# A streaming encoder layer on one core: gate exponentials placed elsewhere in ScalarE's order, tables of the second group in eight buffers between weight slabs, four product stores, one norm buffer per tile

## The reference, cut to what matters

```python
proj = x @ w_in                                   # q | k | v | u, 1024 columns each
att  = band attention of 16 heads over q, k, v    # with a learned bias on distance
ssm  = s5(u)                                      # 64 groups x 64 complex states, GELU, gate
mix  = concat(rmsnorm(att), rmsnorm(ssm)) @ w_out
x1   = layer_norm(alpha * x + mix)
# expert layer: 8 heads, 128 x 128 product keys, 16 experts of each head for each token
q    = x1 @ wq ; s = q . keys
idx  = top 16 of (top 16 of s1 + top 16 of s2) ; g = softmax of these 16 scores
a    = einsum('td,tkd->tk', x1, peer_u[idx])      # 128 dot products of 2048 for each token
y    = einsum('tk,tkd->td', gelu(a) * g, peer_v[idx])
x2   = layer_norm(alpha * x1 + y)
```

## Time and profile before

| | us |
|---|---|
| median of three runs | 4193.71 |
| the profiled execution's own time | 4181.71 |
| its span | 4179.8 |
| TensorE busy (L1418 slabs 1036.9, L1728 products 906.0) | 2642.1 |
| VectorE busy (rows: L1251 1042.8 and 296.5, L1238 724.3) | 2805.5 |
| GpSimd busy | 1239.6 |
| ScalarE busy | 345.2 |
| moved by DMA | 1334.30 MB, mean 319 GB/s |

### The profile page before, as it was taken

One profiled execution on the slowest core, in us unless ns is written; L12 is line 12 of the kernel. 1 busy time (PEld: TensorE's weight loads), 2 busy tenths in 40 slices (PEclk: granted clock), 3 DMA queues, 4 the chain that ended last, 5 costly groups with the idle time before them and its releaser, 6 DMA issues.

```text
span 4179.8 us, 31056 instructions
## 1 busy us (share of the span) xinstructions
PE 2642.1 (63%) x11464; PEld 2042.3 (49%) x11464; DVE 2805.5 (67%) x3300; ACT 345.2 (8%) x808; POOL 1239.6 (30%) x1386
## 2 busy tenths in 40 slices
PE   7989989989668677892988499970999500000000
PEld 6868577845454344551557477860887400000000
DVE  4350211389873888778779886298066598999998
ACT  0110221000001212101010000000000001000000
POOL 2440000012231222222222222023022256777772
PEclk9975579989559555895999799985999855555555
DMA  8653144488996899997999799698699998999997
GB/s 239 223 176 86 58 153 165 149 262 314 353 408 236 311 351 354 373 422 289 422 422 398 313 422 412 230 401 336 209 391 423 400 393 300 409 410 410 408 409 331
DMA packets 291063, 1334.30 MB, mean 319 GB/s; under 512 B 69536, under 2 KB 129472, under 8 KB 139488
## 3 DMA queue, kind: packets, MB, share of 16 engines
q0 software_dynamic: 140432, 952.56, 57.2%
q1 hardware_dynamic: 110384, 365.54, 23.9%
q10 hardware_dynamic: 40096, 14.22, 1.7%
HBM read 1284.43 MB, written 57.20 MB: 321 GB/s over the span
## 4 chain that ended last, share of the span: by engine, by line
DMA 34%; DVE 25%; PE 25%; issue 8%; POOL 6%; ACT 1%; ACTq 1%; SPq 0%; DVEq 0%; POOLq 0%
DMA arena<-in_peer_v,arena 20%; PE low L1418 10%; DVE arena L1238 7%; DVE acc L1251 7%; DMA expert_scratch<-arena 6%; PE low L1728 4%; POOL arena L572 3%; DMA arena<-c_scratch 3%; POOL arena L563 3%; PE low L1522 2%; DMA arena<-in_w 2%; PE low L1506 1%; PE acc L1481 1%; DVE low L1251 1%; DMA arena<-in_peer_u,arena 1%
## 5 line engine op out<-in xcount | busy, mean ns | idle before, releaser
L1251 DVE SCALAR_TENSOR_TENSOR acc<-arena,acc 128x2048 f32<-128x2048 f32 x443 | 1042.8, 2354 | 269.0 <-DMA arena<-in_peer_v,arena 247.3
L1418 PE MATMUL low<-arena 128*128 128x192 f32 (+1 forms) x4096 | 1036.9, 416 | 56.6 <-DMA arena<-in_w 36.0
L1728 PE MATMUL low<-arena 128*128 128x256 f32 x4096 | 906.0, 383 | 232.6 <-ACT arena L800 178.1
L1728 PEld LDWEIGHTS low<-arena 128*128 128x128 f32 x4096 | 779.2, 191 | 359.3 <-issue 193.1
L1418 PEld LDWEIGHTS low<-arena 128*128 128x128 f32 x4096 | 742.2, 195 | 342.3 <-issue 33.6
L563 POOL DMA_INDIRECT arena<-in_peer_v,arena x576 | 558.5, 970 | 1061.8 <-DVE acc L1251 790.5
L1238 DVE SCALAR_TENSOR_TENSOR arena<-arena,acc 128x2048 f32<-128x2048 f32 x320 | 724.3, 2284 | 79.1 <-DMA arena<-in_peer_u,arena 72.7
L563 POOL DMA_INDIRECT arena<-in_peer_u,arena x320 | 320.9, 1003 | 1464.8 <-DVE arena L1238 981.5
L1251 DVE SCALAR_TENSOR_TENSOR low<-arena,low 128x2048 f32<-128x2048 f32 x126 | 296.5, 2353 | 18.4 <-DMA arena<-in_peer_v,arena 15.4
L572 POOL DMA_INDIRECT arena<-expert_scratch,arena x256 | 248.0, 969 | 77.9 <-issue 77.9
L1196 DVE TENSOR_REDUCE arena<-arena 128x8 f32<-128x128 f32 x5 | 1.4, 284 | 236.8 <-ACT arena L780 236.8
(11 more groups left out here) (265 smaller groups left out, 2044.7 us busy)
## 6 DMA issues: line engine op xcount, KB each, us to landing
arena<-in_w SPq DMA_DIRECT2D x128, 1024.0 KB, 6.2
arena<-in_ut SPq DMA_DIRECT2D x128, 1024.0 KB, 17.7
expert_scratch<-arena SPq DMA_DIRECT2D x128, 128.0 KB, 15.0
arena<-bias_scratch SPq DMA_DIRECT2D x16, 640.0 KB, 5.6
arena<-in_peer_v,arena POOLq DMA_INDIRECT x576, 12.2
arena<-toeplitz_scratch SPq DMA_DIRECT2D x64, 128.0 KB, 4.8
arena<-c_scratch SPq DMA_DIRECT2D x64, 128.0 KB, 5.4
bias_scratch<-distance_scratch POOLq DMA_DIRECT2D x1, 5120.0 KB, 25.7
```

The costliest lines, as they stand in the source:

```text
L1251: stt(held, slot[j], wv_, held, ALU.mult, ALU.add).then_inc(used, 1)
L1418: ins = mm(L[n % 2][:, 0:width], wring[n % 2][:, k, :], rhs(k), start=k == 0, stop=k == KT - 1)
L1728: ins = mm(L[j % 4][:, 0:NSD], ud[j % 4][:, k, :], lane(catB, k)[:, P:NB], start=k == 0, stop=k == KT - 1)
```

## The change

It reorders and rebuffers; no arithmetic is added or left out. `gates(t)`, `gate(t)` and `activated` stand at other places of their lists, and the GELU of tile 2 is split in two halves. Group B's state tables (and group A's) get eight buffers, their pairs are done in blocks of four (increments) and eight (output) between slabs. The product store has four stage buffers. Layer norm 1 of group B has a buffer for each tile, with all three inputs loaded ahead; the last norms and sums stand elsewhere.

```diff
+PARTS = [(0, 0, KK), (1, 0, KK // 2), (2, 0, KK // 2), (2, KK // 2, KK // 2)]
...
-        tab = [at(H5 + 512 * j, 512) for j in range(4)]
+        tab = [at(o_ + 512 * j, 512) for o_ in (H5, H6 + D) for j in range(4)]
-        x1s = [at(H8, D), at(H7, D), xhatB, xhatB, xhatB]
+        x1s = [at(H8, D), at(H7, D), xhatB, at(H6, D), at(H6 + D, D)]
-        astg = [at(H2 + D + NSD * j, NSD) for j in range(2)]
+        astg = [at(H2 + D + NSD * j, NSD) for j in range(4)]
@@ SP @@
-            weights(N_VB + 4, 2)
-            for g in range(GP):
+            for g in range(8):
                 g_table(g)
-            weights(N_VB + 6, 2)
+            for b in range(6):
+                if b:
+                    for g in range(4 * b + 4, 4 * b + 8):
+                        g_table(g)
+                if b < 4:
+                    weights(N_VB + 4 + b, 1)
+                else:
+                    weights(N_KB + b - 4, 1)
...
             sp.wait_ge(s_done, 2 * GP)
-            for g in range(4):
+            for g in range(8):
                 y_tables(1, g)
-            weights(N_KB, 8)
+            weights(N_KB + 3, 3)
+            for b in range(3):
+                for g in range(8 * b + 8, 8 * b + 16):
+                    y_tables(1, g)
+                if b < 2:
+                    weights(N_KB + 6 + b, 1)
             weights(N_QB, 2)
-            for g in range(4, GP):
-                y_tables(1, g)
...
-            tokens(2, xinB)
+            for t in range(NGA, NT):
+                tokens(t, x1s[t])
             sp.dma_start(keysB, a["keys_t"]).then_inc(keys_in, 16)
             weights(N_MB + 2, 16)
-            for t in (3, 4):
-                sp.wait_ge(xin_free, t)
-                tokens(t, xinB)
...
+                if j == EB - 12:
+                    early_sums()
@@ ScalarE @@
-            for i in range(8):
+            for i in range(4):
                 out_of(N_KB + i, kT[:, i, NA:T], L[i % 2][:, 0:NB])
-            for b in range(8):
-                act.wait_ge(y_done[1], 4 * b + 4)
+            for b in range(4):
+                act.wait_ge(y_done[1], 8 * b + 8)
...
+                out_of(N_KB + 4 + b, kT[:, 4 + b, NA:T], L[b % 2][:, 0:NB])
-            y_store(1, 8, yscrB, U8B)
-            gates(1)
+            y_store(1, 4, yscrB, U8B)
             act.wait_ge(y_done[1], GP)
-            for i in range(8):
+            for i in range(6):
                 out_of(N_QB + i, qB[:, i, :], L[i % 2][:, 0:NB], DH ** -0.5)
             act.wait_ge(yd_ready, 2)
             nc.scalar.activation(yB, yB, ACT.Gelu).then_inc(gelu_done, 1)
+            for i in range(6, 8):
+                out_of(N_QB + i, qB[:, i, :], L[i % 2][:, 0:NB], DH ** -0.5)
...
+                if v == 4:
+                    gates(1)
...
-            products(0, 12)
+            products(0, 40)
             gates(2)
-            products(12, 60)
+            products(40, 92)
+            activated(2)
+            products(92, EB)
+            activated(3)
             gates(3)
-            products(60, 72)
-            activated(2)
-            products(72, 92)
             gates(4)
-            products(92, EB)
-            ln2(0, 2)
+            ln2(0, 0)
+            ln2(1, 1)
             chunk(0)
             chunk(1)
-            ln2(1, 0)
-            ln2(2, 1)
+            ln2(2, 2)
@@ VectorE @@
             decode(0, nothing)
-            for h in range(PH):
-                rows(2)
-                head(1, h)
-            decode(1, rows)
-            rows(2)
+            rows(36)
...
-            rows_to(72)
-            gate(0)
-            rows_to(96)
-            gate(1)
+            for h in range(PH):
+                rows(3)
+                head(1, h)
+            rows(2)
             dve.wait_ge(y_moved[1], 16)
...
+            dve.wait_ge(y_done[1], GP)
+            decode(1, rows)
+            rows_to(96)
...
+                if v == 8:
+                    gate(0)
+                if v == 16:
+                    gate(1)
...
-            rows(64)
+            rows(50)
             for t in range(NGA, NT):
-                ln1(t, xinB, xhatB, lngB, lnbB, low, rows)
+                ln1(t, x1s[t], x1s[t], lngB, lnbB, low, rows)
                 rows(2)
-            rows(60)
+            rows(50)
             for h in range(PH):
-                rows(min(left // PH, 4))
+                rows(5)
                 head(2, h)
             decode(2, rows)
             rows_to(R_U2 + 4)
-            gate(2)
             for t in (3, 4):
                 for h in range(PH):
                     rows(5)
                     head(t, h)
                 decode(t, rows)
-                rows(8)
-                if t == 3:
-                    gate(3)
-            rows(16)
-            gate(4)
-            rows_to(R_V3)
+            rows_to(R_V2)
+            gate(2)
+            rows_to(R_V2 + KK // 2)
+            gate(3)
+            gate(4)
+            rows(4)
+            dve.wait_ge(early_in, 80)
...
+            ln2(0, 0, rows)
+            rows()
+            ln2(1, 1, rows)
+            rows_to(R_V3 + 4)
+            ln2(2, 2, rows)
@@ TensorE @@
-            for g in range(GP):
-                if g % 4 == 0 and g >= 8:
-                    pe.wait_ge(y_out[1], g // 4 - 1)
...
+            for b in range(4):
+                if b:
+                    pe.wait_ge(y_out[1], b)
+                for g in range(8 * b, 8 * b + 8):
+                    c0 = 1024 + CB * (g % 8)
+                    y_pair(1, g, [low[:, c0 + 512 * g2:c0 + 512 * g2 + CB] for g2 in range(2)], U8B, HsB, CB)
+                slab(N_KB + 4 + b, xb, NB)
...
             for t in range(NGA, NT):
                 if t > NGA:
-                    pe.wait_ge(x1t_out, 4 * t)
+                    pe.wait_ge(res_ready, t)
                 residual(t, mixB, NA, low)
-                pe.wait_ge(res_ready, t + 1)
+            pe.wait_ge(res_ready, NT)
+            for t in range(NGA, NT):
                 turned(t, L[0:2])
```

More of the change, by code:

```diff
@@ L301, in build @@
         k_done, k_out, s_done, s_out = (sem(n) for n in ("k_done", "k_out", "s_done", "s_out"))
-        g_in = [sem(f"g_in{j}") for j in range(4)]
+        g_in = [sem(f"g_in{j}") for j in range(8)]
         t_made = [sem(f"t_made{j}") for j in range(2)]
         h_ready = sem("h_ready")
-        y_in = [sem(f"y_in{j}") for j in range(4)]
+        y_in = [sem(f"y_in{j}") for j in range(8)]
         y_done, y_out, y_stored, y_moved = (
@@ L331, in build @@
         ud_used, a_out = sem("ud_used"), sem("a_out")
-        a_st = [sem(f"a_stored{j}") for j in range(2)]
+        a_st = [sem(f"a_stored{j}") for j in range(4)]
         ln2_in, early_in, late_in = sem("ln2_in"), sem("early_sums_in"), sem("late_x1_in")
@@ L399, in _ @@
                 pair_in(0, m)
-            for g in range(4, GP):
+            for g in range(8, GP):
                 y_tables(0, g)
@@ L497, in _ @@
                 sp.dma_start(x1f[t], x1scr[t]).then_inc(late_in, 16)
-            for k, t in enumerate((2, 0, 1, 3, 4)):
+            for t in range(NT):
                 t0, n = TILES[t]
-                sp.wait_ge(y_ready, k + 1)
+                sp.wait_ge(y_ready, t + 1)
                 sp.dma_start(o["y"][t0:t0 + n, :], x1f[t][0:n]).then_inc(outs, 16)
@@ L586, in _ @@
             pool.wait_ge(idx_ready, NT)
-            for b in range(2):
-                pool.wait_ge(a_st[b], 16 * EB // 2)
+            for b in range(4):
+                pool.wait_ge(a_st[b], 16 * EB // 4)
             for k in range(16):
@@ L770, in scores @@
                 src = acc if t < NGA else low
-                if t == NT - 1:
+                if t == NGA:
                     act.wait_ge(x1_stored, 16 * NT)
@@ L894, in _ @@
                 out_of(N_MB + i, mixB[:, i, :], L[i % 2][:, 0:NB])
-            for t in range(NGA, NT):
-                ln1_stats(t, xhatB)
-                ln1_out(t)
+            ln1_stats(2, x1s[2])
+            ln1_stats(3, x1s[3])
+            ln1_out(2)
+            ln1_stats(4, x1s[4])
+            ln1_out(3)
+            ln1_out(4)
             slabs_out(N_WB, 16, mixB, NB)
@@ L1631, in _ @@
                 slab(N_UB[q], xb, NB)
-            for i in range(6):
+            for i in range(2):
                 slab(N_VB + i, xb, NB)
             pe.wait_ge(u_moved[1], 16 * SL)
-            for g in range(GP):
-                pe.wait_ge(g_in[g % 4], 16 * (g // 4 + 1))
-                if g % 4 == 0 and g >= 8:
-                    pe.wait_ge(s_out, GP + g // 4 - 1)
-                for r in range(2):
-                    for g2 in range(2):
-                        c0 = 2 * CB * (g % 4) + CB * r
-                        ins = mm(L[2 + (g // 4) % 2][hf(g2), c0:c0 + CB],
-                                 GTb[g % 4][:, P * r + 64 * g2:P * r + 64 * g2 + 64], U8B[:, 2 * g + g2, :],
-                                 start=True, stop=True)
-                ins.then_inc(s_done, 1)
-            for i in range(6, 8):
```

(28 more changed lines are left out.)

130 lines of the change are left out of this document (65 added, 65 removed).

## The result

The changed kernel took **4035.37 us** (median of 4 runs, 4029.42 to 4040.64), the kernel before 4193.31 us beside it on the same chip: a ratio of 0.9623 [0.9607, 0.964], 158 us less. Five more runs on another chip gave 4035.59 us and 0.9608 [0.9594, 0.9622]. The forecast was 4000 us in a range from 3935 to 4100, so 35 us too low.

A forecast was written before the change was run, and what follows sets the result against it. DMA was taken to bound the stretch from products to row 640, with stalls from ScalarE's order. Row 640 at 3308 plus a 678 us tail made 3986, -194 us against 4180; from 4193.7 that gave 4000 us, range 3935 to 4100.

The forecast's parts named there:

- The mechanism: From products to row 640: ScalarE's list asks too early and delivers too late, stopping VectorE and TensorE; 208 us lost before.
- The sum in bytes: First product to row 640: 497 MB at 422 GB/s, 1177 us, plus 28 us loss; row 640 at 3308, -188 us.
- rival 1: Half of the 208 us loss comes back at other waits of VectorE's list: +76 us, 4076 us; chance 0.17.
- The first failed step: Between first product and row 640, sums, x1 and norm vectors counted only as about 6.6 MB of loads.
- 128 products take about 890 us: Product stretch: with four stores, neither stores nor four-buffer loads pace TensorE, so the products take about 890 us.
- it covers the wait at row 576: Four stores keep products ahead of VectorE's row 576 (about 3105); at 7.75 us each they would end at 3095.
- Rival 4: Products starve and VectorE stands at row 576 until the last; slower from 9.5 us a product; chance 0.03.
- The start of attention and of the products: Stages before the products: attention 28 us earlier, products at 2103 instead of 2174, 71 us earlier.
- The tail: Behind row 640: two of three norms and three sums leave, so 684 us become 678.
- the forecast's last step: Total: the -194 us from the span is taken from the median 4193.7, 12 us above the profiled execution, giving 4000 us.
- Rival 3: DMA gives only 358 GB/s: row 640 at 3490, the run at 4185 us, no gain; chance 0.04.
- Rival 2: Pairs at 2.4 GHz (-17), none of the 28 us loss stays, scores' wait covered: about 3940 us; chance 0.10.

The follow-up runs named there:

- run 1: Kernel before with only ScalarE's list reordered, the GELU of tile 2 halved and gates 2 to 4 at their new rows; ratio 0.9609.
- Run 4: Changed kernel with two stage buffers and two product stores in flight instead of four; 4036.78 us, ratio 0.9623 to the kernel before.
- run 8: Changed kernel with 14 rows moved ahead of VectorE's wait for the state output and its gating at row 106, not 96; ratio 0.9602 to the kernel before.
- Runs 2 and 5: Kernel before with the norm buffers' part alone, ratio 1.005; kernel before with the state tables' part alone, GELU unsplit, ratio 1.001.
- tables_clean: Kernel before with the state tables' part alone: eight buffers, pairs in blocks between slabs, GELU unsplit, picks unmoved; ratio 1.001.
- gates_only: Kernel before with only ScalarE's new order, the halved GELU of tile 2 and the gates' new rows; ratio 0.9609.

## Why the prediction was right, and where it was not

**The mechanism** was as put: ScalarE's list stopped VectorE and TensorE in turn, and its order is the gain (run 1: 0.9609, 164 of 4200 us; the whole change 158 to 165). The four waits of the earlier trace rows are gone, and none of VectorE for the exponentials took their place.

**The sum in bytes.** 497 MB were forecast from 2103 to row 640; the window gives 1226 us at 406 GB/s, 498 MB. At 422 GB/s that is 1180 us. 28 us of loss were left in the sum; 46 were there. By 422 less what each window shows: 10 us at 2998 to 3060, 18 at 3121 to 3200 (sums and norms, 15 forecast), 15 at 3280 to 3329 (double gathers, 8 forecast), 3 over the rest. The decodes, 5 forecast, lost nothing: they lie before 2998 us, and DMA moved 423 GB/s from 2103 to 2601 and 422 from 2601 to 2998. Row 640 came at 3329 and not 3308. One term of the sum for the kernel before was off: it has 298 rows left at 2174 us, but by its row instructions row 345 ran there, so 295 were left, and its windows give 359 GB/s x 1322 us = 475 MB and not 470. That makes its loss 197 us and not 208; of the forecast only rival 1's price hangs on it.

**The first failed step** is the loads of the early sums, which the sum had only as bytes. They stand in SP's list ahead of slab 117, and TensorE's timeline shows the price:

```profile
2998.31 7.17 PE L1759 MATMUL low<-arena 128*128 128x256 f32 x32 [2.13 <-DMA arena<-in_ut]
3035.58 22.65 PE L1759 MATMUL low<-arena 128*128 128x256 f32 x96 [30.10 <-DMA arena<-in_ut]
```

30.10 us without a slab, and the fourth window of the result has the DMA engines full (1.01) but moving 355 GB/s.

**The second** is "128 products take about 890 us": they took 1018. I took 6.95 us for one from a stretch where the rows stood and laid the 7.75 beside flowing rows to the store. Run 4 shows that it isn't: beside flowing rows a product takes 7.75 us with two stores or four, and TensorE waits for slabs, 112 to 114 us in all. 128 x 7.75 us and the stop of 30 above make the 1018 within some us. Only "it covers the wait at row 576" hung on it, and the sign "products 128 x about 7 us without a gap", which did not come. That cover was nearly gone: last product 3121.0, row 576 at 3132.0, forecast 2995 and 3105. It cost the changed kernel nothing and the next one 33 us (run 8). Rival 4's 9.5 us a product was the price at which all the gain is lost; the waiting begins at (3132 - 2103)/128 = 8.0 us.

**The start of attention and of the products** came out by their steps. `h_ready` 1073 (forecast 1069); pairs and four slabs 1073 to 1214, 141 us (141); query slabs' end 1303 (1296); skip term 1236.9 (1239); gating 1313.4 (1317); layer norm 1 in 53 us (54); the slabs behind it at 1909.7 (1908); first product 2102.6 (2103). But the wait of 49.7 us at L1351 was in the step only by its end and not as a wait: with its slots full, DMA ran at 135 GB/s, a loss of (422 - 135)/422 x 50 = 34 us by bytes that the sum did not see, because it counted from 2103. Run 8 took 23 us off that wait.

**That these marks are worth nothing alone** follows from the sum, since an earlier start with rows owed moves the same bytes; the prediction had the eight and 25 rows owed, but it never said that 71 us earlier products are only a few us of time. Runs 2 and 5 show it: 35 and 31 us earlier at the products, and 20 and 1 us later at row 640.

**The tail** took 699 us and not 678. The order there is not the reason: all the kernels in the table but one have 698 to 703 us, `tables_clean` with the tail of the kernel before among them, and the one with 683 is the profiled execution of before. GpSimd's 468 instructions behind row 640 took 452.20 us in it and 478.72 in `gates_only`, which has the same tail. So the forecast took the tail from an execution whose tail was short; why it was short is not shown. That execution was 12 us below its median, which the forecast's last step added to the total, so if those 12 us lie in the tail, they were in the forecast after all. So the span is off by 42 us (21 + 21) and the median by 35: 12 less, and 6 more for the changed kernel's own profiled execution, which lies under its median.

**The rivals.** Rival 1, half of the loss stays (4076), is out: 46 us stayed. Rival 3 is out: transfers ran at 423 GB/s beside products. The section cited there has about 358; another page of the Trainium skill, "HBM Reference", section "Specifications (TRN2)", says that a core streaming alone measures about 425, which this trace agrees with (423). Rival 2 asked for no loss at all (3940), and no run came near it. Rival 4 is out for the changed kernel, but its place is real (runs 1 and 8).

## What to carry to other kernels

Where engines run lists in a fixed order and the transfers are the measure, count bytes still owed at a mark, not the mark: an earlier start with the same bytes owed turns into a longer stop at the next point where one list waits for another. So look for the instruction whose input is not ready when the list comes to it, or whose output is needed before the list gives it, and cut or move that one first; here one GELU in halves was worth 82 us and the tables alone nothing. And price a shared resource from a stretch with the same neighbours: the product's 6.95 us held only while the rows stood.

## What the runs showed of the hardware that I had not expected

- A product's pace with full DMA did not change with the number of stores in flight: 24 products in 186 us with two and with four. With rows standing they took 6.95 us each, with rows flowing 7.75, both at the full TensorE clock (1.00).
- A busy DMA share is not a rate: 1.01 went with 355 GB/s where the early sums were loaded (2998 to 3060) and with 423 where slabs and rows ran (2415 to 2601).
- Two waits can hide each other: two edits worth nothing alone (0.9602 and 0.9616 against 0.9608 and 0.9623 without them) were worth 30 us together (0.9541).
